# Hybrid encoder layer on one core: order of the first down step, who splits the weights, and two products for the sample

## The reference

```
h = RMSNorm(x)
[q | k | v | glu_a | glu_b | gate_logits] = h @ w_in
A: attention over 128 past positions and the own chunk of 64, 16 query heads, 2 key heads, bias, sink
B: GLU -> causal depthwise conv (31 taps) -> LayerNorm over channels -> swish -> @ w_conv_out
m = sigmoid(gate_A) * A + sigmoid(gate_B) * B ;  x = x + RMSNorm(m @ w_out)
h = RMSNorm(x) ;  x = x + RMSNorm((silu(h @ w_gate) * (h @ w_up)) @ w_down)      # width 2816 inside
```

## Time and profile before

| | us |
|---|---|
| median of 3 runs (lowest, highest) | 3202.87 (3197.35, 3208.68) |
| the profiled execution | 3205.59 |
| its span, first to last instruction | 3203.8 |
| PE, DVE, ACT, POOL busy | 3120.9, 1597.4, 1073.6, 545.7 |
| mean granted TensorE clock | 0.991 |

### The profile page before, as it was taken

One profiled execution on the slowest core, in us unless ns is written; L12 is line 12 of the kernel. 1 busy time (PEld: TensorE's weight loads), 2 busy tenths in 40 slices (PEclk: granted clock), 3 DMA queues, 4 the chain that ended last, 5 costly groups with the idle time before them and its releaser, 6 DMA issues.

```text
span 3203.8 us, 42530 instructions
## 1 busy us (share of the span) xinstructions
PE 3120.9 (97%) x16723; PEld 2655.0 (83%) x16723; DVE 1597.4 (50%) x2819; ACT 1073.6 (34%) x1928; POOL 545.7 (17%) x578
## 2 busy tenths in 40 slices
PE   8999889999999999999999999999999999999998
PEld 6778678878887878888888888888899998899987
DVE  7988755545697741003397762002289765200013
ACT  5666432234355531003255532002245443200012
POOL 3950000000382000000085000000058200100000
PEclk9999999999999999999999999999999999999999
DMA  8864568777654355555655354555555424444443
GB/s 275 291 234 178 193 228 296 282 280 289 231 193 151 131 191 186 187 194 202 220 187 184 119 185 170 186 194 210 185 199 175 148 106 149 146 171 173 177 151 127
DMA packets 176487, 622.65 MB, mean 194 GB/s; under 512 B 20656, under 2 KB 26672, under 8 KB 175776
## 3 DMA queue, kind: packets, MB, share of 16 engines
q1 hardware_dynamic: 175328, 619.53, 54.0%
q10 hardware_dynamic: 960, 0.40, 0.0%
HBM read 480.41 MB, written 139.54 MB: 194 GB/s over the span
## 4 chain that ended last, share of the span: by engine, by line
PE 81%; DVE 3%; DMA 1%; ACT 1%; issue 0%; POOL 0%; SPq 0%; DVEq 0%; ACTq 0%; POOLq 0%
PE PS L810 54%; PE PS L862 7%; PE PS L864 7%; PE PS L863 7%; PE PS L844 2%; PE PS L953 2%; PE PS L973 2%; PE PS L941 1%; DVE PS L1498 1%; PE PS L789 1%; DMA out_y_prompt<-x 1%; DMA w_hi<-hi_dram 0%; DMA u<-in_state 0%; DVE PS L1568 0%; DVE x L1573 0%
## 5 line engine op out<-in xcount | busy, mean ns | idle before, releaser
L810 PE MATMUL PS<-h_hi,w_hi 128*128 128x512 f32 (+1 forms) x3328 | 1065.8, 353 | 10.6 <-DVE u L1764 4.6
L810 PE MATMUL PS<-h_hi,w_lo 128*128 128x512 f32 (+1 forms) x3328 | 1066.7, 353 | 0.0
L810 PE MATMUL PS<-h_lo,w_hi 128*128 128x512 f32 (+1 forms) x3328 | 1055.3, 350 | 0.0
L810 PEld LDWEIGHTS PS<-h_hi,w_hi 128*128 128x128 f32 x3328 | 586.2, 189 | 95.2 <-issue 17.0
L810 PEld LDWEIGHTS PS<-h_lo,w_hi 128*128 128x128 f32 x3328 | 585.6, 189 | 90.8 <-issue 1.6
L810 PEld LDWEIGHTS PS<-h_hi,w_lo 128*128 128x128 f32 x3328 | 586.3, 189 | 81.7
L732 POOL TENSOR_TENSOR y<-y,prod 128x512 f32<-128x512 f32 (+1 forms) x333 | 408.0, 1252 | 185.7 <-ACT prod L1235 172.9
L1498 DVE SCALAR_TENSOR_TENSOR PS<-u,dw,PS 128x512 f32<-128x512 f32 (+1 forms) x604 | 434.0, 766 | 7.0
L1927 DVE TENSOR_TENSOR f<-PS,tmp 128x512 f32<-128x512 f32 (+1 forms) x88 | 61.5, 699 | 673.3 <-PE PS L810 654.6
L862 PE MATMUL PS<-w_hi,f_hi 128*128 128x512 f32 x748 | 297.8, 398 | 5.8 <-DVE f L1927 5.4
L864 PE MATMUL PS<-w_hi,f_lo 128*128 128x512 f32 x748 | 295.4, 395 | 0.0
(11 more groups left out here) (199 smaller groups left out, 3559.0 us busy)
## 6 DMA issues: line engine op xcount, KB each, us to landing
w_lo<-lo_dram SPq DMA_DIRECT2D x372, 512.0 KB, 4.4
w_hi<-hi_dram SPq DMA_DIRECT2D x372, 512.0 KB, 3.4
w_raw<-in_w_stream SPq DMA_DIRECT2D x124, 512.0 KB, 3.8
hi_dram<-w_hi SPq DMA_DIRECT2D x124, 512.0 KB, 3.9
lo_dram<-w_lo SPq DMA_DIRECT2D x124, 512.0 KB, 3.7
x<-in_x_prompt SPq DMA_DIRECT2D x4, 2048.0 KB, 11.9
xs<-in_x_prompt SPq DMA_DIRECT2D x12, 512.0 KB, 5.4
out_y_prompt<-x SPq DMA_DIRECT2D x3, 2048.0 KB, 10.7
```

What stands on the lines that cost most here:

```text
L810: last = nc.tensor.matmul(PS[:, k0 + off, 0:n], w, x[:, k, c0:c0 + n], start=first and k == 0, stop=stop and k == KT - 1)
```

## The change

1. `token_major`: in the first down step the tiles whose first-half bank holds the last up result are taken last, and the wait for that result stands before the first of them.
2. DVE's `split_lo` of steps `S_D - 2` to `S_D` moves behind the up product of that step; in step `S_F - 1` of block 0, `split_hi` and `split_lo` of the tile for `S_F + 1` move behind the second tile's `normed_hi` and `normed_lo`.
3. ACT runs a tiny `Square` before the first tile of x has arrived; DVE takes `gains_in` of tiles 0 and 1 ahead of `scale_rows` of tiles 2 and 3.
4. The sample: its low tokens lie beside its high ones in `h_hi` and `f_hi`. In the first half of out and in all of down, `[hi | lo]` (64 columns) x `w_hi` and hi (32 columns) x `w_lo` replace three products of 128 columns. The lo x hi sums come out on partitions 32 to 63; ACT copies them down, DVE adds them, three times in all. In `down_tail` the sample's tile is taken first.
5. In block 0 POOL makes `w_lo` for g = 35 to 51, and it masks the part of `bias` that unit 12 needs; the other masks move to an earlier step. `tail(0)` is 2 and not 1.
6. At the first unit DVE takes `score_max(0)` before all six `act_lows`; at unit 1 `probs_lo(0)` comes before `query_lo(2)`, and PE transposes unit 0's probabilities after a quarter of the step's products instead of half.

The diff, cut to its core:

```diff
         def tail(b):
-            return 3 if b else 1
+            return 3 if b else 2
+        def apart(s):
+            return S_W <= s < S_W + HALF_W or S_D <= s
+        def in_last_bank(b, tt):
+            k = zbank(b, S_D - 1)
+            return k <= obank(b, 0, tt, True) < k + 1 + ext(b)
+        def lo_by_pool(g):
+            return first_unit(0) + 2 <= g < S_W + 2
...
+                    if lo_by_pool(G(b, s) + 2):
+                        g = s + 2
+                        if s == first_unit(b) + 12:
+                            pool.wait_ge(ttr_done, 4 * 12)
+                            nc.gpsimd.memset(bias[:, :, 0:P], NEG).then_inc(history_off, 1)
+                        pool.wait_ge(w_hi_ok, g + 1)
+                        nc.gpsimd.tensor_tensor(w_lo[:, g % LO, :], w_raw[:, g % LO, :],
+                                                w_hi[:, g % HI, :].bitcast(F32), ALU.subtract).then_inc(w_lo_pool, 1)
...
-                    if k == KT // 2 and turn_halfway is not None:
+                    if k == KT // 4 and turn_between is not None:
...
+                if tt == 4 and apart(s):
+                    both = PS[0:2 * S, bank, :], x_hi[:, kts[kk], T:TX + S], wk[0]
+                    if first:
+                        nc.tensor.matmul(*both, start=True, stop=False)
+                        return nc.tensor.matmul(out, hi, wk[1], start=False, stop=False)
+                    nc.tensor.matmul(out, hi, wk[1], start=False, stop=False)
+                    return nc.tensor.matmul(*both, start=False, stop=last_k)
...
-                    for tt in tts:
+                    for tt in sorted(tts, key=lambda t: in_last_bank(b, t)) if s == S_D and kk == 0 else tts:
+                        if s == S_D and kk == 0 and in_last_bank(b, tt):
+                            result_out(pe, b, S_D - 1)
...
-                places = [(0, NS - 2), (1, NS - 2), (0, NS - 1), (1, NS - 1)]
-                places += [(tt, s) for tt in range(2, tiles(b)) for s in (NS - 2, NS - 1)]
+                first = (4, 0, 1) if ext(b) else (0, 1)
+                places = [(tt, s) for s in (NS - 2, NS - 1) for tt in first]
+                places += [(tt, s) for tt in range(2, 4) for s in (NS - 2, NS - 1)]
...
-                            result_out(pe, b, S_D - 1)
...
+            def low_of_sample(b, half, second):
+                A(tmp[0:S, 1, 0:T], PS[S:2 * S, obank(b, half, 4, second), :], ACT.Copy).then_inc(low_rows, 1)
...
+            A(lsum, neghalf[:], ACT.Square)
...
-                    split_hi(G(b, s) + 2)
+                    if s != S_F - 1:
+                        split_hi(G(b, s) + 2)
...
                     if ext(b) and s == S_W + HALF_W:
                         act.wait_ge(w_used, G(b, s))
+                        low_of_sample(b, 0, 0)
                         stash(b, 0)
...
+            def add_low_of_sample(b, half, second):
+                dve.wait_ge(low_rows, 1 + second + half)
+                out = PS[0:S, obank(b, half, 4, second), :]
+                TT(out, out, tmp[0:S, 1, 0:T], ALU.add).then_inc(rows_added, 1)
...
-            scale_rows(0, 2, 0)
             dve.wait_ge(gains_ld, 16)
             gains_in(0, 0)
+            scale_rows(0, 2, 0)
+            gains_in(0, 1)
             scale_rows(0, 3, 0)
-            gains_in(0, 1)
...
-                    if not S_F <= s < S_D - 2:
+                    if not S_F - 1 <= s <= S_D:
                         split_lo(G(b, s) + 2)
...
-                    if ln == 7:
-                        act_lows(b, range(3))
...
+                            if n == 1:
+                                probs_lo(b, 0)
                             if n % 2 == 1 and n + 1 < units(b):
                                 query_lo(b, n + 1)
                             if n == 0:
-                                act_lows(b, range(3, 6))
-                            if 0 < n <= units(b):
+                                act_lows(b, range(6))
+                            if 1 < n <= units(b):
                                 probs_lo(b, n - 1)
```

More of the change, by code:

```diff
@@ L48 @@
 YS = T + HIST
-WIN0 = TX - P
-SR = P - S
 NEG = -1e30
@@ L405, in turned, with lo_made @@
             return PS[:, k:k + 2, :].rearrange("p a (c t) -> p (a c) t", t=P)
+        def lo_by_pool(g):
+            return first_unit(0) + 2 <= g < S_W + 2
+        def lo_made(eng, g):
+            if lo_by_pool(g):
+                eng.wait_ge(w_lo_pool, g - first_unit(0) - 1)
+            else:
+                eng.wait_ge(w_lo_ok, sum(not lo_by_pool(i) for i in range(g + 1)))
         def first_in(ring, slot):
@@ L853, in token_products @@
                 g, half, i = G(b, s), (s - s0) // n_half, (s - s0) % n_half
-                t0 = tok0(b, tt)
-                out = PS[:, obank(b, half, tt, s0 == S_D), :]
-                hi, lo = x_hi[:, kts[kk], t0:t0 + P], x_lo[:, kts[kk], t0:t0 + P]
+                bank = obank(b, half, tt, s0 == S_D)
+                out = PS[rows(tt), bank, :]
+                hi = x_hi[:, kts[kk], toks(tt)]
+                lo = x_hi[:, kts[kk], TX:TX + S] if tt == 4 else x_lo[:, kts[kk], toks(tt)]
                 wk = [w[:, g % n, kk * T:(kk + 1) * T] for w, n in ((w_hi, HI), (w_lo, LO))]
@@ L904, in down_tail @@
                                               kk, tt)
-                    if tt == tiles(b) - 1:
+                    if tt == 3:
                         last.then_inc(w_used, 1)
+                    elif tt == 4 and s == NS - 1:
+                        last.then_inc(sample_done, 1)
                     elif s == NS - 1:
@@ L1177, in first_squares @@
                         act.wait_ge(sq0_ok, m)
+                    if tt == 4:
+                        act.wait_ge(rows_added, 1 + second)
                     A(tmp[r, 0, 0:T], o_half(b, 0, tt, second), ACT.Square,
@@ L1456, in _ @@
                 for tt in range(tiles(b)):
-                    if tt < tiles(b) - 1:
+                    if ext(b) and tt == 0:
+                        act.wait_ge(sample_done, 1)
+                        low_of_sample(b, 1, 1)
+                        act.wait_ge(rows_added, 3)
+                    if tt < 3:
                         act.wait_ge(d_done, out_tile(b, tt))
-                    else:
+                    elif tt == 3:
                         act.wait_ge(w_used, G(b, NS - 1) + 1)
@@ L1565, in residual @@
                 dve.wait_ge(prs_ok, m + 1)
+                if tt == 4:
+                    dve.wait_ge(rows_added, 1 + 2 * second)
                 o = [o_half(b, half, tt, second) for half in range(2)]
@@ L1816, in _ @@
                         sum_squares_of_tiles(b)
+                    if ln == 5 and b == 0:
+                        dve.wait_ge(bias_in, 16 * 8)
+                        masks(bias[0:P // 2, :, P + P // 2:2 * P], bias[P // 2:P, :, 0:P // 2])
+                    if ln == 5 and b == 1:
+                        dve.wait_ge(bias_in, 16 * 16)
+                        masks(bias[P // 2:P, :, 0:P // 2])
                     if ln == 6:
@@ L1899, in _ @@
                             late_lo(b, i)
+                    if ext(b) and s in (S_W + HALF_W, S_D + HALF_D):
+                        add_low_of_sample(b, 0, s > S_D)
                     if s == S_F - 1:
```

83 lines of the change are left out of this document (42 added, 41 removed).

## The result

The changed kernel takes 3175.72 us (median of 4 runs, 3172.80 to 3179.35), the kernel before 3205.69 beside it (4 runs); the ratio is 0.992 with an interval of 0.9904 to 0.9937, so 20 to 31 us less. The forecast was 3164, its range 3150 to 3186. The profiled execution took 3172.80, its span is 3171.0: 32.8 less than in the trace of before.

What follows compares the result with a forecast made beforehand. TensorE, busy for 97% of the span, bounds the kernel; only fewer products or less of its 83 us standing can help. Gains sum to 38.5: 3205.6 - 38.5 = 3167.1, less 2.7 for the median: 3164 us, range 3150 to 3186.

Steps and rivals of the forecast that it cites:

- sample's products: Out and down steps: 52 fewer products, 11.2 us before the tail, less 1.9 tail, 0.6 stash, 0.2 hand-overs: 8.5 gained.
- first down step: Four blocks: taking tiles with free banks first covers the wait for the last up product; gain 5.4 us, at least 4.
- POOL's `w_lo`, conv stage: Block 0's conv steps: six splits, 7.6 us, and waits for `w_hi` leave DVE; gain 8.5 us, 3 to 11.
- first units, block 0: Waits for first maximum (4.05 us) and `pt_lo` (1.3) go, 1.8 given to a new wait; gain 3.5, 2 to 5.3.
- first units, blocks 1 to 3: The 1.27 us wait nearly goes three times, `probs_lo(0)` being ahead of the query; gain 3.4, 1.3 to 3.6.
- out to FFN, block 0: `tail(0)` = 2 sums tile 0 4.2 us earlier; gain 4.3 with a trifle for the order, 2 to 10.
- start, with GLU of block 0: Kernel start: earlier ACT table load moves DVE's last subtraction before PE's first product forward; gain 0.9 us, 0 to 1.3.
- clock: Half-clock stretches behind long waits may go with the waits; three counted, gain 4 us, between 0 and 7.
- the slower rival: DVE stands through POOL's 17 splits, 4.3 us each, 2.9 beyond the slack: 49 us lost, 3224 in all; chance 0.05.
- the slack of 1.4: Conv stretch: DVE has 39.2 us to do against PE's 47.9, leaving 1.4 us for each POOL split.
- The price by stretching: DVE operations under a POOL split take 1.6 to 1.7 times as long, about 0.9 us lost per split.
- the price of the rival: Sample's products: about 60 groups with three stationary shape changes each, 180 x 0.10 = 18 us, giving 3182; chance 0.09.

Runs made afterwards that it cites:

- three products: Changed kernel, but the sample has three products of 32 columns in all steps, without low sums, copy or addition: 3187.55 us, 0.9955 of before.
- two distances: Changed kernel, h_hi's rows 2176 bytes apart in blocks 0 to 2 and 2304 in block 3, same memory: 3162.95 us, 0.9881 of before.
- wide rows: Kernel before, with h_hi's rows 2304 bytes apart and not 2176, added columns unused: 3212.40 us, 1.0036 of before.
- the hole: Kernel before, with 1024 unused bytes behind h_hi so only later buffers move, rows still 2176 bytes apart: 3203.17 us, 1.0006 of before.
- 2432 bytes: Changed kernel with h_hi's rows 608 tokens (2432 bytes) apart, 32 columns of each row unused: 3165.27 us, 0.9887 of before.

## Why the prediction came out as it did

The range and the sign held. The forecast itself was 12 us low on the median, 5.7 on the profiled execution (38.5 forecast, 32.8 measured), and 3175.72 lies outside the 3150 to 3174 that were the forecast's own; it is in the range by the room left for the rivals. Term by term, the measured size from the table of stages, lost clock included where it fell, rounded:

| term | forecast | measured |
|---|---|---|
| sample's products | 8.5 | 8.4 = 11.0 (out and down, against three products) - 2.6 (behind PE's last product) |
| first down step | 5.4 | 6.1 (gaps) |
| POOL's `w_lo`, conv stage | 8.5 | 7.8 = 5.5 (PE's standing) + 2.2 (clock) |
| first units, block 0 | 3.5 | -1.2 |
| first units, blocks 1 to 3 | 3.4 | 5.2 = 1.0 + 1.0 + 3.2 (some 1.7 of it clock) |
| out to FFN, block 0 | 4.3 | 3.8 |
| start, with GLU of block 0 | 0.9 | 1.2 = -0.1 (PE's first product) + 1.3 (GLU) |
| clock | 4 | in the rows above and below |
| GLU and FFN, blocks 0 to 2 | none | -11.8 |
| GLU and FFN, block 3 | none | 3.8 |
| down, all blocks, not by the two products | none | 7.4 = 5.4 (some 1.6 of it clock, block 0) + 2.0 |
| out and the norms, blocks 1 and 2, and small rest | none | 2.2 |

**The largest error** is a term that the prediction did not have: the wider rows of `h_hi` were costed at nothing, without a word. The only thing said of the layout was that the sample's low tokens lie beside its high ones. GLU of blocks 1 and 2 and FFN of blocks 0 to 2 became 11.8 us longer; with the half clock evened out (10.9 us of PE's work there before, 6.8 after, half of it lost) that is 13.9, and the pairs that differ in the rows alone give the same in that way: 14.0 for the changed kernel against two distances, 13.7 for wide rows against the hole. The wide rows alone, in the kernel before, cost 0.36% in all. A part came back elsewhere: the last block is faster with these rows, and in down (block 1) the next product starts 226.3 ns after one of `w_lo` x `f_hi` and not 230.0, which the wide rows of `h_hi` alone do not give (229.8). `f_hi` and `f_lo` have new row widths as well; that these are the reason was not tried.

That the total came within the range is luck in part: this loss of some 14 us, which nobody had counted, stood beside gains that nobody had counted either, 7.4 in down, 3.8 in the last block, and 8 more of the clock than forecast (part of the other rows).

**First units, block 0.** A gain of 3.5 was forecast, a loss of 1.2 came. The new wait was foreseen and sized at 1.8 by six `act_lows` of 1.03; it was 5.3. The order alone makes 2.9 of it (DVE splitting again), and 2.4 come because two of the `act_lows` stood for nearly whole POOL splits. A stretch at half clock follows it; the other two lines are the half clock that is left in front of FFN of block 0 and in FFN of block 1:

```profile
233.40:240.30 6.90, 5.72 (x18) 4.87 (x19) 4.66 (x16) 2.49 (x7) 0.00 (x0) 0.51 0.40 165
...
428.00:434.90 6.90, 6.22 (x30) 5.69 (x29) 6.07 (x8) 3.02 (x4) 0.74 (x2) 0.51 0.42 152
1189.20:1192.60 3.40, 3.40 (x16) 3.40 (x17) 3.37 (x5) 1.80 (x2) 0.00 (x0) 0.50 0.43 174
```

This is the slower rival's mechanism: DVE stood to the end of a split, for 1.5 us of a 2.4 us split in the conv steps, over 2 at the first unit. It stayed near the slack of 1.4 and well below the 3.1 from which it would have decided. The price by stretching (1.6 to 1.7 times, so 0.9 per split) was the wrong form. The Trainium skill's "SBUF — State Buffer", section "Who interferes with whom", has the right one: the engine that started first keeps the shared pair for its whole instruction. The trace agrees, with 345.00 against 344.98: an operation that takes 0.17 us elsewhere paid 1.6.

**Products.** The count and the 0.233 were right, and columns change at no cost. 52 products are 12.1 us; 11.0 came out of the stages, and the wait for the stash, 1.1 for 0.4, is the 0.6 of the sum. (There are 52 groups of the sample's products, two in each of 26 steps, not about 60; only the price of the rival went by that number.) On a change of tiling the Trainium skill's "TensorEngine Tiling (Array Packing)", section "Key Properties", says that TensorE is drained; with 32 and 64 columns of 128 rows the starts here stay 0.22 to 0.24 apart, so that rule put no price on this kernel. At the end ACT's copy, DVE's addition and the first residual (timelines):

```profile
3152.00 0.59 ACT L1239 ACTIVATE tmp<-PS 32x512 f32<-32x512 f32 x1 [3.41 <-PE PS L893]
...
3152.62 0.69 DVE L1631 TENSOR_TENSOR PS<-PS,tmp 32x512 f32<-32x512 f32 x1 [2.57 <-ACT tmp L1239]
...
3155.33 0.75 DVE L1620 SCALAR_TENSOR_TENSOR ostash_d<-ostash_d,prs,gp 128x512 f32<-128x512 f32 x1 [2.02 <-POOL prs L722]
...
3168.68 0.33 SPq L619 DMA_DIRECT2D out_y_sample<-x  x1
```

The chain of residuals is about as long as in the earlier trace rows (13.4 us, 13.6 there), but 10.80 and not 8.16 us of the kernel now lie behind PE's last product. The sum has that as the 1.9 of the tail, the 0.2 for the hand-overs, and the four products of the tail (0.9) that it did not count as a gain: 3.0 forecast, 2.6 measured. Even the kernel with three products has that 2.6 (10.79 behind PE's last product), so it is the sample's place at the head of the tail that costs it, not the copies.

**Conv.** 7.8 is near the forecast of 8.5, but not in the way that was worked out. 7.6 us of splits left DVE, and some 6.2 came back: in this stretch four negations (L1663) of 0.17 us took 1.64 to 1.77 beside POOL's splits, which is why DVE is at 45.4 and not 39.2. What went is the standing that the prediction named beside the work and gave no number: DVE's waits for ACT's `w_hi`, 8.7 us before and 0.9 after. And 2.2 of the 7.8 is PE's own work, shorter because the clock there went from 0.97 to 1.00.

**First down step, tail, clock.** The first two are near their forecast. Half-clock stretches held 46.3 us of PE's work before and 22.1 after, so some 12 us were won in this execution and not 4; in the other variants of the changed kernel 22 to 39 are left, and this is a part of what makes runs differ. At the start, DVE's last subtraction ended 0.9 earlier as forecast, yet PE's first product came at 18.78 and not before: PE was not done with its own work ahead of it. Its transposes of x took 0.42 us each. In the two variants where the product came at 17.75 and 17.91 they took 0.27; in the others 0.42 again, and it came at 18.4 to 18.8. The 1.3 of GLU in block 0 is within what that stage varies by, so the profiled execution does not show the 0.9; those two variants do.

**The signs.** The wait for the last up product is gone, the 17 splits take 2.38 to 2.90 us, the starts stay at 0.233 and the residuals follow without a hole, as was said. DVE in the conv stretch was to be below 42 us and is at 45.4; the first full FFN step of block 0 was to start 24 to 26 us behind out's end and starts after 26.8 (29.8 before); PE's waits for `h_lo` (2.4) and for ACT (1.8) on the way there are as before.

## What to carry to other kernels

When a diff adds columns to a buffer that TensorE streams, its row distance is a term of the sum: compare the spacing of products in stages that should not have changed. Work that is given to POOL can be paid by the DVE instruction that meets it, by the rest of the POOL instruction and not by a share of it, so look at which operations DVE runs when POOL will start: a negation of four numbers paid 1.6 us here, the maximum's operation on PSUM nothing. What the move gave was a wait taken out of DVE's queue, so count the waits ahead of an instruction with its time. And cut both traces at the same products before explaining a total; gains and losses of some 12 us stood side by side here, and half-clock stretches of 3.4 us fell in other stages from one execution to the next.

## What was not expected of the hardware

The distance of the moving operand's rows changes the pace of TensorE: with 2176 and 2432 bytes 24 products of 512 columns take 5.52 us, with 2304 they take 5.60. The place of the later buffers is not the reason: with 2176 bytes it is 5.52 behind the hole too, and the kernel with two distances differs from the changed one in the rows alone. In the last block, whose 544 columns stream as two pieces of 272, 2304 is the better one: at full clock a product of `h_hi` x `w_lo` in FFN is followed by the next after 124.2 ns, and after 126.7 with 2176 and with 2432 bytes. FFN took 267.1 us in the changed kernel, 269.8 in the one before and 270.7 with 2432 bytes, some 1.7 of the last at half clock. Why, stays open; one would need more distances, with everything else fixed.
